# Transposed inverse updated two chunks at a time from one stationary matrix, with parts of the beginning, the output phase and the end in another order

## The reference, cut to what matters

```python
h = rmsnorm(x, g_pre); p = h @ w_in          # 2048 x 8208, one projection
mixer A: dilated window attention, 8 heads x 128 (prompt, and samples against a cache)
mixer B: gated DeltaNet, 8 heads, per chunk of tokens:
    a_mat = strict_lower(kbeta @ k.T) * decay
    t_mat = triangular_solve(a_mat + eye, eye)   # the inverse of a unit triangular matrix
    u, w = t_mat @ v_beta, t_mat @ (kbeta * exp(gcum))
    scan over the chunks with state S
y = concat(o_a * silu(z_a), o_b * silu(z_b)) @ w_out
out = x + rmsnorm(y, g_post)
```

## Time and profile before

| | |
|---|---|
| runs | 1253.79 us median of 3 (1251.59 to 1254.14) |
| profiled execution | 1254.01 us, span 1252.1 us |
| granted TensorE clock, mean | 0.992 |
| PE | 1215.2 us busy (97%) |
| PEld | 1132.5 us (90%) |
| DVE | 803.7 us (64%) |
| ACT | 514.1 us (41%) |
| POOL | 301.8 us (24%) |
| DMA | 151.56 MB, mean 121 GB/s |

### The profile page before, as it was taken

The page is one execution under the profiler, slowest core; times in us unless marked ns, Lnnn a source line. Parts: engine busy times, 40 slices in busy tenths (PEclk is TensorE's granted clock), DMA queues, the critical chain, the costliest instruction groups (busy, mean ns, idle before and its releaser), DMA issues.

```text
span 1252.1 us, 25551 instructions
## 1 busy us (share of the span) xinstructions
PE 1215.2 (97%) x8814; PEld 1132.5 (90%) x8814; DVE 803.7 (64%) x1958; ACT 514.1 (41%) x1365; POOL 301.8 (24%) x275
## 2 busy tenths in 40 slices
PE   4999999999999999999999999999999998999997
PEld 4999999999999899989998999899999998999996
DVE  6476477656765676577657756775677575565544
ACT  6443334533453445344533543354345445322210
POOL 1114121411232123212321231123213221222211
PEclk9999999999999999999999999999999998999998
DMA  7232453244325432543154325432544274322253
GB/s 240 89 102 59 141 162 102 62 139 161 102 62 156 151 102 62 159 142 109 53 174 134 106 57 180 129 101 56 188 119 127 72 235 125 107 67 90 79 202 137
DMA packets 79646, 151.56 MB, mean 121 GB/s; under 512 B 12353, under 2 KB 22242, under 8 KB 77986
## 3 DMA queue, kind: packets, MB, share of 16 engines
q1 hardware_dynamic: 78542, 149.31, 38.5%
q10 hardware_dynamic: 1024, 1.07, 0.4%
HBM read 132.20 MB, written 17.27 MB: 119 GB/s over the span
## 4 chain that ended last, share of the span: by engine, by line
PE 81%; DVE 9%; issue 4%; ACT 4%; DMA 2%; SPq 1%; DVEq 0%; ACTq 0%
PE PJ L602 17%; PE PJ L598 11%; PE PJ L599 10%; PE PJ L600 10%; PE PJ L603 8%; PE MX L805 3%; PE MX L786 2%; DVE memx L1545 1%; PE MX L797 1%; PE MX L729 1%; PE MX L709 1%; PE PJ L918 1%; PE MD L857 1%; PE MD L896 1%; PE PJ L919 1%
## 5 line engine op out<-in xcount | busy, mean ns | idle before, releaser
L602 PE MATMUL PJ<-h,w_hi 128*128 128x512 f32 x1110 | 416.9, 412 | 0.2 <-DVE memx L1381 0.2
L1915 POOL TENSOR_TENSOR w_lo<-w_raw,w_hi 128x512 fp32r<-128x512 f32 x160 | 215.6, 1348 | 829.9 <-ACT w_hi L990 829.9
L598 PE MATMUL PJ<-h,w_hi 128*128 128x264 f32 (+1 forms) x1248 | 365.9, 293 | 1.2 <-ACT memx L1020 1.2
L599 PE MATMUL PJ<-h,w_hi 128*128 128x264 f32 (+1 forms) x1248 | 353.8, 283 | 0.0
L600 PE MATMUL PJ<-h,w_lo 128*128 128x264 f32 (+1 forms) x1248 | 353.5, 283 | 0.0
L603 PE MATMUL PJ<-h,w_lo 128*128 128x256 f32 x1110 | 310.7, 280 | 0.0
L602 PEld LDWEIGHTS PJ<-h,w_hi 128*128 128x128 f32 x1110 | 208.9, 188 | 43.8 <-DVE w_lo L1350 1.7
L990 ACT ACTIVATE w_hi<-w_raw 128x512 fp32r<-128x512 f32 x320 | 196.7, 624 | 108.2 <-PE PJ L600 76.5
L598 PEld LDWEIGHTS PJ<-h,w_hi 128*128 128x128 f32 x1248 | 235.3, 189 | 5.4 <-issue 3.9
L599 PEld LDWEIGHTS PJ<-h,w_hi 128*128 128x128 f32 x1248 | 235.6, 189 | 1.6
L600 PEld LDWEIGHTS PJ<-h,w_lo 128*128 128x128 f32 x1248 | 234.3, 188 | 0.0
(11 more groups left out here) (325 smaller groups left out, 1826.0 us busy)
## 6 DMA issues: line engine op xcount, KB each, us to landing
w_raw<-in_w_in SPq DMA_DIRECT2D x256, 256.0 KB, 2.7
w_raw<-in_w_out SPq DMA_DIRECT2D x64, 256.0 KB, 2.8
kv<-in_cache_win_k SPq DMA_DIRECT2D x24, 512.0 KB, 4.7
kv<-in_cache_win_v SPq DMA_DIRECT2D x16, 512.0 KB, 4.2
out<-memx SPq DMA_DIRECT2D x16, 260.0 KB, 3.8
mem<-in_x_prompt SPq DMA_DIRECT2D x4, 1024.0 KB, 10.1
S<-in_state_delta SPq DMA_DIRECT2D x8, 512.0 KB, 3.4
out<-S SPq DMA_DIRECT2D x8, 512.0 KB, 2.9
```

The costliest lines, as they stand in the source:

```text
L598: pe.matmul(ps, wh, h_hi[:, k, tok], start=k == 0, stop=False)
L599: pe.matmul(ps, wh, h_lo[:, k, tok], start=False, stop=False)
L602: pe.matmul(both, wh, h2[:, :, k, tok], start=k == 0, stop=False)
L1915: pool.tensor_tensor(w_lo[:, par, 4 * q:4 * q + 4, :], w_raw[:, q, :, :], w_hi[:, par, 4 * q:4 * q + 4, :].bitcast(F32), ALU.subtract).the ...
```

## The change

- Levels 1 to 5 of `mix_b`: the update of T takes two matmuls of 128 columns instead of four of 64. Chunk j and chunk j + 2 share one stationary matrix `b_W[:, j]`, whose odd blocks of rows come from `b_U` of the one and whose even blocks from the other. DVE makes it (`both_rows`: one TENSOR_SCALAR and one SCALAR_TENSOR_TENSOR of 128x256), for level 1 right behind level 0 of T, for levels 2 to 5 behind the subtractions of the level before. PE waits for `mix_W`. A table `odd_rows` is loaded.
- Beginning: the first block of x_prompt is loaded ahead of `g_pre`; ACT takes the first `x_hi` ahead of `ba_hi` and of the third block's root.
- Rows 10 and 11: loaded by ACT's queue right behind the first four `g_hi`, no longer by SP behind its other loads.
- Output phase: ACT squares (`y_squares`) the first five tiles, DVE only adds them up, and the fifth tile's scaling stands behind the first sum.
- End: the sample's transposes stand between those of the second token block, no longer ahead of it.
- A semaphore is merged (`zero_cols` into `cw_ok`).

```diff
@@ SP
+            sp.dma_start(xin[:, 0, :], x_prompt[0, 0:P, :]).then_inc(x_in[0], 16)
             for n in range(2):
                 sp.dma_start(g_bc[n], g_pre[0, n * WA:(n + 1) * WA].partition_broadcast(P)).then_inc(s["g_in"], 16)
-            sp.dma_start(xin[:, 0, :], x_prompt[0, 0:P, :]).then_inc(x_in[0], 16)
...
+            sp.dma_start(odd_rows[:].rearrange("p a n -> p (a n)"), c_odd).then_inc(s["s_loaded"], 16)
...
             def late_rows():
-                sp.wait_ge(s["gated_b"], NH)
-                for k in (10, 11):
-                    load_row(k)
                 yield
@@ PE, mix_b
-                    for c in chunks if n < LEVELS - 1 else (2, 3):
-                        last = pe.matmul(blocks(mx(3)[:, c, :], n, c // 2), b_U[:, c, :],
-                                         blocks(b_Y[:, c % 2, :], n, c // 2), start=True, stop=True)
+                    if n < LEVELS - 1:
+                        pe.wait_ge(s["mix_W"], (LEVELS - 2) * h + n)
+                        for j in range(2):
+                            last = pe.matmul(crossed(mx(3), n, False, j), b_W[:, j, :],
+                                             b_Y[:, j, :].rearrange("p (k a s) -> p a k s", a=2, s=1 << n),
+                                             start=True, stop=True)
+                    else:
+                        for c in (2, 3):
+                            last = pe.matmul(blocks(mx(3)[:, c, :], n, 1), b_U[:, c, :],
+                                             blocks(b_Y[:, c % 2, :], n, 1), start=True, stop=True)
@@ PE, end
-            for c in (0, NC, 1, 2, 3):
-                n = P if c < NC else NB
+            for c in range(NC):
                 for b in range(4):
...
+                    if c == 1:
                         if b == 3:
                             pe.wait_ge(s["fin_rs"], 1)
+                        for k in range(4):
+                            last = pe.transpose(Y_S[b][:, k * P:(k + 1) * P], y_ch[:, 4 * b + k, TP:TT], ident[:])
+                        last.then_inc(s["y_T"], 1)
@@ ACT
             x_rstd(0, 0)
             x_rstd(1, 1)
+            x_hi(0)
             ba_hi()
             x_rstd(2, 2)
-            x_hi(0)
             x_hi(1)
...
             for k in range(4):
                 g_hi(k)
+            act.wait_ge(s["gated_b"], NH)
+            act.wait_ge(s["gB_out"], 16 * (NH - 1))
+            act.wait_ge(s["gA_out"], 16 * (NH - 1))
+            for k in (10, 11):
+                act.dma_start(g_row[k], scratch_g[k]).then_inc(row_in[row_group(k)], 16)
...
-            with repeat(act, 0, (KT - PARTS - 1) // 2) as i:
+            for n in range(2 * PARTS + 2):
+                tok = TOKENS[n % 2]
+                act.wait_ge(s["proj_sb"], 2 * T_O + n + 1)
+                if n > 3:
+                    act.wait_ge(s["sq_y"], n - 3)
+                act.activation(sq_part[n][:, tok], (cq if n < 2 else sz)[:, tok], ACT.Square).then_inc(s["y_squares"], 1)
+                if n % 2 == 1 and 1 < n:
+                    hi(T_O + PARTS + 2, 1, n // 2 - 1)
+            for q in range(NQ):
+                hi(T_O + PARTS + 3, 0, q)
+            with repeat(act, 1, (KT - PARTS - 1) // 2) as i:
@@ DVE
+            def both_rows(n):
+                link(dve.tensor_scalar(b_W[:], b_U[:, 2:4, :], odd_rows[:, 1, n:n + 1], None, ALU.mult))
+                dve.scalar_tensor_tensor(b_W[:], b_U[:, 0:2, :], odd_rows[:, 0, n:n + 1], b_W[:], ALU.mult,
+                                         ALU.add).then_inc(s["mix_W"], 1)
...
                     dve.tensor_tensor(t, t, all_blocks(mx(0)[:, 2:4, :], 0, odd), ALU.subtract).then_inc(
                         s["mix_T"], 1)
+                dve.wait_ge(s["mix_U0"], 3 * h + 3)
+                both_rows(1)
                 yield from idle(2)
...
                     dve.tensor_tensor(t, t, tz, ALU.subtract).then_inc(s["mix_UT"], 1)
+                    if n < LEVELS - 2:
+                        dve.wait_ge(s["mix_UT"], UTS * h + 2 * n - 1)
+                        both_rows(n + 1)
```

More of the change, by code:

```diff
@@ L252, in build @@
         kvl = sb("kvl", [4 * NB, 2, P])
+        b_W = sb("b_W", [P, 2, P])
+        odd_rows = sb("odd_rows", [P, 2, LEVELS])
         terms = sb("terms", [4 * NB, NB + 2])
@@ L295, in build @@
         MD = ctx.enter_context(nc.psum_tensor("MD", [P, 2, TP], F32))
+        sq_part = [(ez, xz)[n // 2 % 2] for n in range(2 * PARTS + 2)]
         Y_S = [PJ[0:NB, 0, :], PJ[0:NB, 1, :], MD[0:NB, 1, :], MD[0:NB, 0, :]]
@@ L331, in build @@
             "act_chain dve_chain "
-            "zero_cols cw_ok crow_out conv_ok conv_sig kv_silu q_silu "
+            "cw_ok crow_out conv_ok conv_sig kv_silu q_silu "
             "hg_ok mix_T1 mix_ss mix_lnrk mix_rs mix_scal mix_gb mix_tok mix_kbT_ps mix_kbT mix_arg mix_D "
-            "mix_kk mix_qk mix_A mix_QK mix_B mix_U0 mix_T_ps mix_T mix_Y_ps mix_Y mix_Z mix_UT ch_kS ch_r "
+            "mix_kk mix_qk mix_A mix_QK mix_B mix_U0 mix_T_ps mix_T mix_Y_ps mix_Y mix_Z mix_W mix_UT ch_kS ch_r "
             "ch_v_ps ch_v ch_S_ps ch_o_ps ch_S ch_o1 ch_o o_sq on_rs o_n o_T z_sig_b z_ok_b gated_b gB_out S_out "
@@ L961, in _ @@
             pe.wait_ge(s["proj_sb"], 2 * (T_O + KT))
-            for c in (0, NC, 1, 2, 3):
-                n = P if c < NC else NB
+            for c in range(NC):
                 for b in range(4):
-                    if c == NC:
-                        out = Y_S[b]
+                    if c > 0:
+                        pe.wait_ge(s["y_out_ok"], 4 * (c - 1) + b + 1)
+                    for k in range(4):
+                        last = pe.transpose(MX[:, b, k * P:(k + 1) * P], y_ch[:, 4 * b + k, c * P:(c + 1) * P], ident[:])
+                    last.then_inc(s["y_T"], 1)
+                    if c == 1:
                         if b == 3:
                             pe.wait_ge(s["fin_rs"], 1)
[L969 to L975, removed]
+                        for k in range(4):
+                            last = pe.transpose(Y_S[b][:, k * P:(k + 1) * P], y_ch[:, 4 * b + k, TP:TT], ident[:])
+                        last.then_inc(s["y_T"], 1)
         @block.scalar
@@ L1865, in _ @@
                 dve.wait_ge(s["proj_ps"], 2 * (T_O + PARTS - 1) + half + 1)
-                dve.tensor_copy(sz[:, TOKENS[half]], PJ[:, half, 0:WIDTH[half]]).then_inc(s["proj_sb"], 1)
+                dve.tensor_copy(cq[:, TOKENS[half]], PJ[:, half, 0:WIDTH[half]]).then_inc(s["proj_sb"], 1)
             lo(T_O + PARTS + 1, 0, 0)
[L1868 to L1887, removed]
+            def y_sum(n):
+                tok = TOKENS[n % 2]
+                dve.wait_ge(s["y_squares"], n + 1)
+                if n > 1:
+                    dve.wait_ge(s["sq_y"], n - 1)
+                dve.tensor_tensor(acc[:, tok], acc[:, tok], sq_part[n][:, tok], ALU.add).then_inc(s["sq_y"], 1)
@@ new lines, in _ @@
+            for n in range(2, 2 * PARTS + 2):
+                j, half = n // 2 - 1, n % 2
+                tok = TOKENS[half]
+                dve.wait_ge(s["part_sb"], 2 * j + half + 1)
+                if half == 0:
+                    dve.wait_ge(s["rest_ps"], j + 1)
+                elif j < NQ - 1:
+                    dve.wait_ge(s["w_used"], 3 * (T_O + PARTS) + j + 1)
+                else:
+                    dve.wait_ge(s["proj_ps"], 2 * (T_O + PARTS) + 2)
+                if n > 3:
+                    dve.wait_ge(s["y_squares"], n - 1)
+                dve.tensor_tensor(sz[:, tok], PJ[:, half, 0:WIDTH[half]], y_ch[:, j, tok], ALU.add).then_inc(
+                    s["proj_sb"], 1)
+                dve.wait_ge(s["proj_sb"], 2 * T_O + n + 1)
+                dve.tensor_scalar(y_ch[:, j, tok], sz[:, tok], vecT[:, j:j + 1], None, ALU.mult)
+                if n < 4:
+                    dve.tensor_scalar(y_ch[:, PARTS, TOKENS[n - 2]], cq[:, TOKENS[n - 2]], vecT[:, PARTS:PARTS + 1], None,
+                                      ALU.mult)
+                y_sum(n - 2)
+                if n == 3:
+                    lo(T_O + PARTS + 1, 0, 2)
@@ L1888, in _ @@
+            for n in range(2 * PARTS, 2 * PARTS + 2):
+                y_sum(n)
             ch.end(1)
@@ L1905, in _ @@
                     x = xres[c][:, b * TP:(b + 1) * TP]
-                    dve.wait_ge(s["y_T"], 4 * (c + 1 if c > 0 else 0) + b + 1)
+                    dve.wait_ge(s["y_T"], (b + 1, 5 + 2 * b, 13 + b, 17 + b)[c])
                     dve.scalar_tensor_tensor(x, MX[:, b, :], fin[:, c:c + 1], x, ALU.mult, ALU.add).then_inc(
```

25 lines of the change are left out of this document (11 added, 14 removed).

## The result

| | before | changed |
|---|---|---|
| median | 1252.69 us (1250.78 to 1254.14) | 1259.95 us (1258.84 to 1260.88) |
| ratio | | 1.0055, 95% interval 1.0038 to 1.0071 |
| span of the profiled execution | 1252.1 us | 1258.8 us |
| PE busy | 1215.2 us | 1199.9 us |
| DVE busy | 803.7 us | 844.3 us |

The change makes the kernel slower: by 7.3 us between the medians, 0.55% by the ratio. The forecast was 1250.7, in a range of 1233 to 1257; the time lies 3 us above that range, in a direction to which the prediction had given 0.15.

What follows compares the result with a forecast made beforehand. The prediction took PE, busy 97%, as the bound: passes without a gap plus some 14 us of waits and 6 of low clock. 1254.0 − 30.8 (gains) + 16.4 + 2.6 + 8.5 = 1250.7 us, range 1233 to 1257.

Steps and rivals of the forecast that it cites:

- Pairing, −18.0: T's update, levels 1 to 5: 160 passes saved at 0.1125 us each, a pass costing the same with half the columns.
- The rival by columns: PE's passes cost by their columns, so pairing saves nothing: 1268.7 us, chance 0.02.
- q_silu, +16.4: DVE at level 1: `both_rows(1)` and POOL's turns delay `q_silu` by 2.2 us in seven heads, plus head 0.
- head 0's share: Part of the `q_silu` delay put on head 0: +1.0 us, between 0 and 2.2.
- Levels 2 to 5, "nothing is waited for": `b_W` made behind a level's subtractions is ready before the next level's update, so no wait: 0 us.
- Level 6's Y, +2.6: `both_rows(5)` pushes level 5's subtractions, so PE waits at level 6's Y: 0.37 us in seven heads.
- Clock, +8.5: Low clock behind PE's 2.4 us gaps at `q_silu`: five of seven heads at 1.7 us, between 0 and 23.8.
- Beginning, −0.9: Start of the kernel: earlier first `x_hi` shortens PE's idle time by 0.9 us, between 0 and 2.6.
- Rows 10 and 11, −6.2: Loads on ACT's queue remove PE's 3.43 us gap and 2.8 us of low clock, or nothing if late.
- tiles, −4.8: First five output tiles: PE's 3.1 us wait for the first addition and 1.7 us of low clock go.
- end, −0.9: End: part of DVE's 1.50 us wait for the sample's transposes between the first two blocks goes.
- The slower rival: The `q_silu` stall comes with two low clock stretches after each gap: 1266.0 us, chance 0.08.

Runs made afterwards that it cites:

- e10: Changed kernel with pairs only in levels 1, 3 and 4, level 1's `b_W` a slot later, levels 2 and 5 with four matmuls of 64 columns: 1228.69 us.
- e11: e9 with level 5 in the old form, so pairs in levels 1 to 4 only: 1226.19 us.
- e4: Changed kernel, only POOL's `lo` of slot 34 in heads 1 to 7 waits for `q_silu`: 1245.73 us.
- e9: e1 with POOL's second `lo` of that tile also waiting for `d_vec`: 1228.63 us.
- e8: Changed kernel with the beginning's old order, `g_pre` ahead of the first block and the first `x_hi` behind the third root: 1264.12 us.
- e12: Changed kernel with squares, scalings and sums of the first output tiles on DVE in the old order: 1266.04 us.
- e7: Changed kernel with rows 10 and 11 loaded by SP's queue again: 1263.44 us.
- e5: Changed kernel with the old update of T (four matmuls of 64 columns) and without `both_rows`, all reorders kept: 1239.27 us.
- e1: Changed kernel with `both_rows(1)` one slot later, behind `q_silu`: 1239.64 us.

## Why the prediction was wrong

**Pairing, −18.0.** Right: 0.43 to 0.45 a level and head in the trace, 3.3 to 3.5 us a level in e10 and e11. That a pass of 64 columns costs what one of 128 does holds. The rule by columns counts the columns alone, but every pass of this kernel has a weight load of its own (8654 of each), and a projection pass of 264 columns costs no more than 0.12 either (232.24 to 232.36 in the earlier trace rows). The rival by columns, 1268.7, is out, though its time lies no further from the result than the forecast's: a time alone proves nothing of its cause.

**q_silu, +16.4.** Right in size and in mechanism; head 0's share was a guess that came near: 7 x 2.15 and, in head 0, 0.8 plus the restart, 16.0. The turns stand in the rows one by one, and e4 shows that POOL's `lo` is 1.08 of each 2.35.

**Levels 2 to 5, "nothing is waited for".** This step failed, and it alone is more than the miss. It asked who needs `b_W`, and `b_W` was indeed never waited for. It didn't ask what stands on DVE behind `both_rows(2)`: twelve small instructions with a due time of their own, which had ended 0.3 us ahead of POOL's `lo`. A push of 0.75 put the last of them under a turn of 1.27. PE waits 1.3 us at 873 in all eight heads: 10.5 us, about 12 with the restarts (e9 gets 11 back). The slack to PE, 1.2 us, just covered the push of 0.78 (233.12 to 233.90, from `both_rows(2)` to the next instruction) and the 0.45 by which the saved passes bring PE sooner; the slack to POOL's `lo`, 0.3 us, did not. The forecast had priced the same rule, in the same head, at the first place and forgot it at the second.

**Level 6's Y, +2.6.** The right push at the wrong receiver. `both_rows(5)` costs 1.67 and not 0.73, as POOL holds its first instruction, and PE feels it earlier, at 885: 4.4 us, 5 with the restarts. (By its own rows the term was 252.35 − 252.03 = 0.32 a head, 2.2 and not 2.6.)

**Clock, +8.5.** Four low stretches of 3.4 us at 0.5, some 6 to 7 us, for five of 1.7. The price of one was right, the count a guess that came near. Its upper bound was not what it said: the 3.4 a head are twice 1.7, while the stretch behind the 3.43 us gap costs 2.8. That a 2.35 us gap can leave the clock alone shows in three heads; why those is open.

**Beginning, −0.9.** Too small. The first projection starts 2.6 us sooner (41.44 for 43.99), and undoing it costs 4.2; in e8's trace PE's two waits ahead of the transposes are 3.5 us longer (13.0 and 5.1 for 10.5 and 4.1). x_hi started at 14.38 for 19.82, and POOL's two `ba_lo` did not hold DVE's `h_lo`: with ACT's `w_hi` later, they came at 16.86 and were through at 17.41, before `h_lo` (17.42), at under 0.3 each: their 1.03 before was itself a lost turn. Timeline of the changed kernel:

```profile
14.38 2.04 ACT L1072 ACTIVATE h<-MX 128x512 fp32r<-128x512 f32 x4
...
16.86 0.55 POOL L2030 TENSOR_TENSOR w_lo<-memx,w_hi 128x64 fp32r<-128x64 f32 x2 [16.42 <-ACT w_hi L1079]
...
17.42 2.47 DVE L1435 TENSOR_TENSOR h<-MX,h 128x512 fp32r<-128x512 f32 x4
```

**Rows 10 and 11, −6.2; tiles, −4.8; end, −0.9.** The rows are issued at 1043.79 by ACT and nobody waits for them, but undoing it costs 3.5, not 6.2: with SP's queue the wait is 2.2 here, for 3.4 before, and has 1.0 in the changed kernel. The tiles gave 6.1; in e12's trace the waits in the output phase are 2.0 longer. In neither e7 nor e12 does the clock fall behind these waits (1.00 from 1050 to 1240), so the 2.8 and the 1.7 of low clock in the two terms are not shown where the forecast had them; what those traces have is the low stretch behind the last sum. The end wasn't tried alone. With the beginning these terms sum to 12.8 forecast and 13.4 measured (e5), so their errors cancel: the total is right by luck as much as by reasoning.

In sum: 1252.7 − 13.4 − 17.6 (pairs) + 16.0 + 12 + 5 + 6.5 = 1261, measured 1260. Against these terms the forecast lacked 12 at level 2 and 2.4 at level 5, and had 2 too much for the clock and 0.6 too little gain for the reorders; its base, the profiled execution, was 1.3 above this median. No term had the low stretch behind the last sum (1233.00 in the earlier trace rows): PE waits 1.73 us there in both kernels, and the changed one's trace stays at 1.00, which is 1.7 us of luck in the measured time. The slower rival named the clock; the loss came from a wait that no rival had.

## What to carry to other kernels

When instructions are put on an engine that is not the bound, list everything behind them on that engine up to its next idle time, and for each result the slack to its reader; who reads the new result is only half of the question. Where two engines take turns, the slack of a chain ends where the other engine's next long instruction starts, here 0.3 us, not where the reader comes. Two remedies are worth trying at each place. At level 1 moving the work got 20 us and holding POOL back 14; at level 2 moving it got nothing, and holding back the long, uncritical instruction until the short chain was over got 11, with one wait on POOL.

## What was not expected of the hardware

A DVE instruction of 8 columns takes 1.13 us instead of 0.17 when POOL's `lo` has started first, and the next one, behind POOL's mask, 0.59: both end with POOL's instruction, so here the cost of losing a turn is what is left of the other's instruction, whatever the own work. The trace of before has it already, beside the `lo` of the earlier trace rows that starts at 223.24, where nobody waits for the result:

```profile
223.29 1.25 DVE L1692 TENSOR_TENSOR dd<-memx 128x8 f32<-128x8 f32 x1
```

A forecast could have read there what a chain of such instructions risks.

And equal gaps of 2.35 us in PE's work left the granted clock at 0.5 for 3.4 us in four heads and at 1.00 in three, while gaps of 1.27 to 1.30 us (e1, e4) left it at 1.00 in every head. The gap of 1.73 us behind the last sum was followed by a low stretch in the kernel before and by none in the changed one.
